# A two-block transformer on one core: later output pieces in the mixers, turns behind the next sums, and a different share of the convolution's taps

## The reference

```
def token_mixer(h, w_in, g_moba_out, g_dsa_out, w_out, cos, sin):
    proj = h @ w_in                                   # 1024 -> 3656
    mq, mk, mv, dq, dk, dv, qi, ki, wi = jnp.split(proj, offs, axis=-1)
    ...                                               # partial rope
    o_moba = moba_attention(mq, mk, mv)               # 8 heads of 64, causal (one block of 256)
    o_dsa = dsa_attention(dq, dk, dv, qi, ki, wi)     # 8 heads; each query keeps its 64 best keys
    o = jnp.concatenate([rms_norm(o_moba, g_moba_out), rms_norm(o_dsa, g_dsa_out)], axis=-1)
    return o @ w_out

def first_block(...):
    for l in range(2):
        h = rms_norm(x, g_pre_mix[l]) * (1.0 + sc_m) + sh_m
        y = token_mixer(h, ...)
        x = x + gt_m * rms_norm(y, g_post_mix[l])
        h = rms_norm(x, g_pre_ffn[l]) * (1.0 + sc_f) + sh_f
        y = conv_glu_ffn(h, ...)
        x = x + gt_f * rms_norm(y, g_post_ffn[l])

def _conv_module(h, w1, b1, wdw, bdw, lng, lnb, w2, b2):
    a, gt = jnp.split(h @ w1 + b1, 2, axis=-1)
    u = a * jax.nn.sigmoid(gt)
    u = depthwise_conv(u, wdw) + bdw                  # 31 taps per channel
    u = jax.nn.silu(_layernorm(u, lng, lnb))          # over the 1024 channels
    return u @ w2 + b2
```

## Time and profile before

| | |
|---|---|
| median of 3 runs | 2647.69 us (2647.56 to 2654.18) |
| time of the profiled execution | 2649.03 us |
| its span from first to last instruction | 2646.9 us |
| mean granted clock of TensorE | 0.981 |
| PE busy | 2513.1 us, 95% |
| DVE / ACT / POOL busy | 66% / 41% / 17% |
| mixer 0, mixer 1 | about 50 to 240, 430 to 624 us |
| convolution module | about 1206 to 1400 us |

### The profile page before, as it was taken

One profiled execution on the slowest core, in us unless ns is written; L12 is line 12 of the kernel. 1 busy time (PEld: TensorE's weight loads), 2 busy tenths in 40 slices (PEclk: granted clock), 3 DMA queues, 4 the chain that ended last, 5 costly groups with the idle time before them and its releaser, 6 DMA issues. The chain is left out here.

```text
span 2646.9 us, 35239 instructions
## 1 busy us (share of the span) xinstructions
PE 2513.1 (95%) x13530; PEld 2102.8 (79%) x13530; DVE 1739.2 (66%) x2566; ACT 1077.4 (41%) x1824; POOL 447.4 (17%) x466
## 2 busy tenths in 40 slices
PE   4899999989999999999989999999999999999998
PEld 3678997678988878878648888888888888777997
DVE  6977886966995785775865464665565765345454
ACT  3445554446554222226755322224322224334543
POOL 1101111001121121113842112101112110000111
PEclk9989999999999999999999999999999999999999
DMA  7544785534774563551102243452343353222462
GB/s 304 203 161 149 265 324 207 203 128 171 246 267 153 166 203 125 191 183 65 64 24 72 88 172 144 146 183 89 135 167 119 143 182 117 89 77 71 156 196 95
DMA packets 118294, 413.02 MB, mean 156 GB/s; under 512 B 13552, under 2 KB 17776, under 8 KB 118128
## 3 DMA queue, kind: packets, MB, share of 16 engines
q1 hardware_dynamic: 117568, 409.06, 44.4%
q10 hardware_dynamic: 560, 1.72, 0.2%
HBM read 409.68 MB, written 1.05 MB: 155 GB/s over the span
## 5 line engine op out<-in xcount | busy, mean ns | idle before, releaser
L1102 PE MATMUL ps<-hH,sh 128*128 128x256 f32 (+1 forms) x2560 | 842.6, 329 | 7.2 <-DVE sl L1672 2.8
L1103 PE MATMUL ps<-hL,sh 128*128 128x256 f32 (+1 forms) x2560 | 835.7, 326 | 0.0
L1104 PE MATMUL ps<-hH,sl 128*128 128x256 f32 (+1 forms) x2560 | 835.6, 326 | 0.0
L1672 DVE TENSOR_TENSOR sl<-raw,sh 128x1024 fp32r<-128x1024 f32 x534 | 650.6, 1243 | 119.3 <-ACT sh L1381 118.7
L1381 ACT ACTIVATE sh<-raw 128x1024 fp32r<-128x1024 f32 x534 | 540.2, 1039 | 391.5 <-PE ps L1104 317.9
L1686 DVE CUSTOM_DVE_ANT_0 mjunk<-raw,cB,V 128x1024 bf16<-128x1024 f32 x384 | 546.5, 1423 | 32.3 <-DMA C<-in_cst 8.4
L1102 PEld LDWEIGHTS ps<-hH,sh 128*128 128x128 f32 x2560 | 483.0, 189 | 59.5 <-issue 9.3
L1103 PEld LDWEIGHTS ps<-hL,sh 128*128 128x128 f32 x2560 | 481.0, 188 | 48.6 <-issue 1.7
L1104 PEld LDWEIGHTS ps<-hH,sl 128*128 128x128 f32 x2560 | 481.0, 188 | 48.1
L2167 POOL TENSOR_TENSOR uLl<-F,uHh 128x256 fp32r<-128x256 f32 (+1 forms) x132 | 165.8, 1256 | 981.9 <-ACT uHh L1561 851.7
L1102 PE MATMUL ps<-sh,uHh 128*128 128x512 f32 x792 | 314.2, 397 | 14.8 <-DVE sl L1672 14.6
(11 more groups left out here) (170 smaller groups left out, 2284.9 us busy)
## 6 DMA issues: line engine op xcount, KB each, us to landing
raw<-in_w SPq DMA_DIRECT2D x756, 512.0 KB, 4.4
raw<-in_w SPq DMA_DIRECT2D x16, 256.0 KB, 3.7
cB<-in_rpb SPq DMA_DIRECT2D x64, 64.0 KB, 2.7
X<-in_x ACTq DMA_DIRECT2D x1, 1024.0 KB, 11.8
X<-in_ctx SPq DMA_DIRECT2D x1, 1024.0 KB, 8.0
out<-X SPq DMA_DIRECT2D x2, 512.0 KB, 2.6
raw<-in_w SPq DMA_DIRECT2D x2, 288.0 KB, 6.0
cB<-in_c ACTq DMA_DIRECT2D x1, 512.0 KB, 5.6
```

What stands on the lines that cost most here:

```text
L1102: self.e.matmul(out, lh, rh, start=start, stop=False)
L1103: self.e.matmul(out, lh, rl, start=False, stop=False)
L1104: return self.e.matmul(out, ll, rh, start=False, stop=stop)
L1672: self.e.tensor_tensor(lo[:, 0:w], raw[:, 0:w], hi[:, 0:w].bitcast(F32), ALU.subtract).then_inc(self.sems["w_lo"], 1)
```

## The change

It reorders steps of the plan, and moves some of the convolution's work between engines. PE's rows of the program go from 11,805 to 11,804; DVE's stay at 2,049.

1. `index_scores`: each tile's eight rounds are four steps of `aside` with two rounds each, before two steps of four.
2. Output pieces are written to the columns of tiles 2 and 3 of h, which nothing else uses there, and are issued four rounds after their row (before: two, and none before the projection's end), one in a round. The 5-fold warm-up before the second half of the output product is gone, and row 1's DSA piece is issued behind the first evacuation.
3. `gate_half` puts the held turns out before `rms_close`; `norm_tile` has `early`, which puts the splits before the scale. The last tile of each is thus evacuated and squared before the earlier tile's turn. `down` does so only for l = 0 by `lead`, and the neighbourhood attention's output product by `early`.
4. The convolution: ACT and POOL do seven taps of a group before its next step (five of the last; before four), the last two groups have other shares, 8 warm-ups stand between the last two means (before 12 behind the last), and the groups whose hL is made by DVE are 0, 3, 5, 7 (before 1, 3, 5, 7; the rest is POOL's).

```diff
--- before.py
+++ after.py
@@ -21,7 +21,9 @@
 HALF = KF // 2
 NEG = -1e30
 GONE = -3e38
-SHARE = [(5, 11)] * 2 + [(6, 10)] * 4 + [(9, 10), (13, 8)]
+SHARE = [(5, 11)] * 2 + [(6, 10)] * 4 + [(7, 9), (13, 5)]
+HL_V = (0, 3, 5, 7)
+FIRST = [7] * 7 + [5]
 
 UNIT = 1024
 RAW = 8
@@ -213,13 +215,15 @@
     def xs(self, t, h):
         return ("x", t, h, self.x_at[(t, h)])
 
-    def norm_tile(self, hid, t, AB, s, st=None, wide=False, lag=0):
+    def norm_tile(self, hid, t, AB, s, st=None, wide=False, lag=0, early=False):
 
         if st is None:
             st = self.rms_open(self.xs(t, 0), D)
         self.rms_more(st, self.xs(t, 1))
         self.first_parts(lag)
         self.rms_close(st, 2)
+        if early:
+            self.second_parts()
         ys = [self.place("S", j) if wide else self.next("PT", 2) for j in range(2)]
         self.add("scale", t=t, st=st, ys=ys, xs=[self.xs(t, 0), self.xs(t, 1)])
         self.second_parts()
@@ -263,7 +267,7 @@
         self.left(b)
         self.add("hsplit", p=p)
 
-    def down(self, w, act, nk, k0, tiles, done, bias=None, c0=0):
+    def down(self, w, act, nk, k0, tiles, done, bias=None, c0=0, lead=False):
 
         if bias is not None:
             self.flush()
@@ -288,7 +292,7 @@
                         self.second_parts()
                     self.add("down", unit=n, ks=ks, tiles=[(i, (t, banks[i]))], last=i == len(tiles) - 1,
                              full=banks[i] if u == len(taken) - 1 else None, **common)
-                if i and len(tiles) == 2:
+                if i and lead:
                     self.first_parts()
                     self.second_parts()
                 done(t, half, banks[i])
@@ -331,6 +335,7 @@
         if half == 0:
             st2[("y", t)] = y
             return
+        self.first_parts()
         self.rms_close(st2[t], 2)
         for j in range(2):
             x0 = self.xs(t, j)
@@ -338,7 +343,7 @@
             self.add("gate2", y=(st2[("y", t)], y)[j], t=t, j=j, st=st2[t], x0=x0, x1=self.xs(t, j))
             if j == 0:
                 st = self.rms_open(self.xs(t, 0), D)
-        self.norm_tile(hid, t, AB, 0, st)
+        self.norm_tile(hid, t, AB, 0, st, early=True)
 
     def gated(self, t, half, b, gid, fast):
         f = self.next("F", 3)
@@ -402,7 +407,7 @@
                 self.left(b)
 
         h2 = self.new()
-        late, ripe = [], [False]
+        late = []
 
         def out(it, ob):
             kd, i = it["kind"], it["i"]
@@ -412,14 +417,13 @@
             self.rms_close(st, 1)
             self.add("oscale", mid=mid, kd=kd, i=i, st=st)
             A = ("V", "g_dsa_out" if kd else "g_moba_out", (l,), 0)
-            late.append([2, lambda: self.o_piece(("O1", i, 512 * kd), ("os", mid, kd, i), 4 * kd, i, A, "v", h2)])
+            late.append([4, lambda: self.o_piece(("O1", i, 512 * kd), ("os", mid, kd, i), 4 * kd, 2 + i, A, "v", h2)])
 
         def pieces(all=False):
-            for x in list(late):
+            for x in late:
                 x[0] -= 1
-                if ripe[0] and (x[0] < 0 or all):
-                    late.remove(x)
-                    x[1]()
+            if late and (all or late[0][0] < 0):
+                late.pop(0)[1]()
 
         def stream(kind):
             items = []
@@ -488,7 +492,6 @@
                     turn(("stg", stg, cb), list(range(g0, g0 + 4)), sc, g0 // 4)
             pending.append(go)
         assert not pending and not moba
-        ripe[0] = True
         gid = self.gates_later("w_ada", l, 2, ("g_post_mix", (l,)), 1)
 
         w, act, tiles = ("w_out", l), ("h", h2), [0, 1]
@@ -496,7 +499,7 @@
         units = [(kp, half) for kp in range(4) for half in range(2)]
 
         def part(kp, half, n, which, last, full=None):
-            self.add("down", unit=n, ks=[2 * kp, 2 * kp + 1], tiles=[(i, (i, banks[half][i])) for i in which], last=last,
+            self.add("down", unit=n, ks=[2 * kp, 2 * kp + 1], tiles=[(2 + i, (2 + i, banks[half][i])) for i in which], last=last,
                      full=full, act=act, nk=KD, bias=False)
 
         def take(kp, half):
@@ -516,8 +519,8 @@
             self.pace()
         self.flush()
         AB = [ab_next()]
-        self.warm(5)
-        pieces(True)
+        while len(late) > 1:
+            pieces(True)
         hid = self.new()
         st2 = {}
         self.rate = RATES["out"]
@@ -526,10 +529,9 @@
             for half in range(2):
                 for kp in (2, 3):
                     part(kp, half, taken[(kp, half)], [i], i == 1, banks[half][i] if kp == 3 else None)
-                if half:
-                    self.first_parts()
-                    self.second_parts()
                 self.gate_half(i, half, banks[half][i], gid, AB, hid, st2)
+                if i == 0 and half == 0:
+                    pieces(True)
                 self.pace()
         self.u_at += 1
         self.add("u_free", u=self.u_at)
@@ -545,8 +547,7 @@
         steps = []
         for i in range(2):
             steps += [lambda i=i: (some(i, 0), some(i, 1)), lambda i=i: (some(i, 2), some(i, 3))]
-            steps += [lambda i=i: self.add("rank", mid=mid, i=i, lo=0, hi=4),
-                      lambda i=i: self.add("rank", mid=mid, i=i, lo=4, hi=8)]
+            steps += [lambda i=i, lo=lo: self.add("rank", mid=mid, i=i, lo=lo, hi=lo + 2) for lo in range(0, 8, 2)]
         self.turn_at["S"] = -1
         self.aside[0:0] = steps
 
@@ -589,7 +590,7 @@
             AB[0] = ab_next()
         self.aside += [lambda: None] * (5 if l else 9) + [later]
         self.down(("w_down", l), ("u1", fid), KF, 0, [0, 1],
-                  lambda t, half, b: self.gate_half(t, half, b, gid, AB, hid, st2))
+                  lambda t, half, b: self.gate_half(t, half, b, gid, AB, hid, st2), lead=l == 0)
         self.flush()
         self.u_at += 1
         self.add("u_free", u=self.u_at)
@@ -693,9 +694,9 @@
             self.add("cglu_v", c=c, ba=ba, s=s, up=ups[c], cid=cid)
             self.left(ba, bu)
             if c:
-                tap_p(c - 1, 4, SHARE[c - 1][1])
+                tap_p(c - 1, FIRST[c - 1], SHARE[c - 1][1])
                 tap_v(c - 1, 5, 31)
-            tap_p(c, 0, 4)
+            tap_p(c, 0, FIRST[c])
             if 0 < c < 7:
                 tap_w(c + 1)
 
@@ -721,14 +722,13 @@
             group(c, ba, bu)
             if c == 5:
                 AB = [ab_next()]
-        tap_p(7, 4, SHARE[7][1])
         bias = ("conv_b_pw2_2", (0,))
         mean(5)
         taps(7)
         tap_v(7, 5, 31)
         mean(6)
+        self.warm(8)
         mean(7)
-        self.warm(12)
         b = self.bank()
         for c in range(KD):
             self.add("ln_sq", c=c, m=total[0], b=b, f=self.next("F", 3), cid=cid)
@@ -825,7 +825,7 @@
         def done(t, half, b):
             self.gated(t, half, b, gid, half == 1)
             if half:
-                self.norm_tile(h2, t, AB, t // 2, early[t], t % 2 == 1, 1)
+                self.norm_tile(h2, t, AB, t // 2, early[t], t % 2 == 1, 0, True)
             else:
                 early[t] = self.rms_open(self.xs(t, 0), D)
 
@@ -2054,7 +2054,7 @@
         self.wait_ge(self.got("rstd", s["cid"]))
         self.e.tensor_tensor(self.flat(c), self.flat(c), self.buf(s["b"])[:, :], ALU.mult).then_inc(self.sems["v_ps"], 1)
         self.done("v_ps", ("cn", s["cid"], c), *([("left", s["b"])] if c == KD - 1 else []))
-        if c % 2:
+        if c in HL_V:
             self.hc_lower(s, "v_sb")
 
     def hc_lower(self, s, sem):
@@ -2195,7 +2195,7 @@
             self.done("p_sb", ("left", f), *([("ap", cid, c)] if j == SHARE[c][1] - 1 else []))
 
     def ln_out(self, s):
-        if s["c"] % 2 == 0:
+        if s["c"] not in HL_V:
             self.hc_lower(s, "p_sb")
```

## The result

The changed kernel takes 2642.49 us (median of 20 runs, 2633.04 to 2648.00), the kernel before in the same rounds 2649.28 us (20 runs, 2644.94 to 2654.18). The ratio is 0.9973, with a 95% interval of 0.9964 to 0.9981: some 7 us faster, where 9.4 was forecast. The profiled execution took 2643.63 us, its span went from 2646.9 to 2641.8.

What follows compares the result with a forecast made beforehand. PE was taken as the bound, busy 2513.1 of 2646.9 us, with DVE the bound in the front. Terms -8.5 - 5.5 + 8.5 - 0.6 - 3.3 = -9.4 took the profiled 2649.0 to 2639.6, median about 2638.3; range 2628 to 2649.

Steps and rivals of the forecast that it cites:

- the forecast's 45: The 45% chance given to the forecast's own case, with a range of 2631 to 2644 us.
- Ranks, -8.5: Mixer fronts: ranks in four steps bring evacuations of q and k earlier, saving 4.0 us in mixer 0, 4.5 in mixer 1.
- The walk: Mixer 0's front: DVE's new order with old durations; PE transposes the fifth MoBA item 4.4 us earlier, the next gives 0.4 back.
- The forecast sign for the ranks: Mixer fronts: PE's waits on L1482 and L1847, 12.4 us before, would fall under 4.
- ranks only move: Rival, 20%: with DVE 96% busy in the front, a removed wait returns at a later item; 2646.8 us.
- DSA starts, -5.5: Starts of the DSA rounds: shorter waits for the copy of PT save 4.5 us, less half clock 0.5 a mixer.
- Ends, +8.5: End of attention: later pieces cost 2.3 and 1.8 us in the mixers, half clock behind an uncovered wait 4.4.
- Convolution, -3.3: Convolution: new shares, warm-ups moved between the last means, and group 0's hL on DVE together save 3.3 us.
- (a): Convolution's taps: with new shares the last CB is ready 0.2 us earlier; PE's wait of 7.76 stands.
- (b): Convolution's warm-ups: sums of squares start 5.6 us earlier but half clock costs 3.1, so -2.5, from -0.8 to -4.2.
- (c): Convolution: hL of group 0 takes 0.69 us on DVE for 1.26 on POOL, saving 0.6 us.
- Neighbourhood attention, -0.6: Neighbourhood attention: evacuation, squares and splits go ahead of PE's 1.87 us wait for a scale, saving 0.6 us.

Runs made afterwards that it cites:

- E1: The changed kernel with the ranks back in two steps of four rounds; 2644.42 us, 0.9988 of the kernel before.
- E11: E6 with MoBA row 0's piece two rounds behind its row and ranks in two steps of four rounds; 2636.56 us, 0.9970 of the kernel before.
- E3: The changed kernel with the turns ahead of the last tile's evacuation and squares again, everywhere; 2645.53 us, 0.9995 of the kernel before.
- E4: The changed kernel with all of the convolution's part undone; 2644.97 us, 0.9991 of the kernel before.
- E6: The changed kernel with only DSA's output pieces issued as before, behind the 5-fold warm-up; 2629.41 us, 0.9941 of the kernel before.
- E7: The changed kernel with a 10-fold warm-up inside the 5.4 us wait ahead of the last sums; 2637.92 us, 0.9975 of the kernel before.
- E9: E6 again, unaltered, on another chip; 2632.33 us, 0.9946 of the kernel before.
- E12: E6 without the 5-fold warm-up ahead of row 1's piece; 2638.15 us, 0.9974 of the kernel before.
- E5: The changed kernel again, unaltered, on another chip; 2643.89 us, 0.9990 of the kernel before.
- E8: The changed kernel with the convolution's 12-fold warm-up back behind the last mean; 2644.49 us, 0.9995 of the kernel before.
- E2: The changed kernel with all output pieces issued as before, and the 5-fold warm-up; 2637.75 us, 0.9963 of the kernel before.

## Why the prediction came out as it did

The time was near by luck: errors nearly as large as the whole forecast cancelled. In the first trace the ranks gave 8.3 us less than their term and the convolution 1.1 less. The DSA starts gave 4.8 more, the ends cost 4.4 less, and the neighbourhood attention gave 2 more. Stretches that the change doesn't touch took some 6 back. The gain was 6.8 us, or 2.4 on the other chip. The 57% for a gain of over 0.3% was too much even by the prediction's own account: it counted 40 of the forecast's 45 as below 2639.8, though the forecast's range goes on to 2644.

- **Ranks, -8.5: wrong.** They gave 0.9 in mixer 0 and cost 0.7 in mixer 1; E1 and E11 find nothing to tell from zero. The step that failed is "PE ... transposes that item at about 134.1 rather than 138.47 ... The next item gives 0.4 back". That item was transposed at 137.53, and the next one is 0.9 earlier too. The walk followed masks and transposes, and left out that the products with v need copies of PT from DVE. The first of these stood behind two rounds, the two operations that end the rank and a modulation step. PE, 7.5 us ahead until then, waits 3.85 us for it at 126.73 (4.56 in mixer 1), and runs at half clock for 3.6 us behind it. The forecast sign for the ranks, waits on L1482 and L1847 under 4 us, came true (1.6) without the gain. The rival "ranks only move" named it: DVE works 46.9 of 48.6 us there before and after.
- **DSA starts, -5.5: right in kind.** They gave 5.3 and 5.0. The waits themselves went from 6.1 to 4.5 us in mixer 0 and from 5.9 to 3.8 in mixer 1, 3.7 instead of 4.5. The other 6.6, for which I took 1.0, is mostly the granted clock, which rose from 0.66 to 0.86 in mixer 0; a part is that row 1's division no longer stands behind row 0's piece on DVE, which the ends pay for. That share is not the edit's alone: with the same order of instructions there, six of the experiments' kernels (E3, E4, E6, E7, E9, E12) show 0.80, E1, E5 and E8 0.86. E3, E4 and E7, whose order is that of the changed kernel up to the last division, gained 5.4 us there, just the forecast, instead of 10.3.
- **Ends, +8.5: right in place, too large.** The wait of 5.6 was 5.40, that of 1.1 was 0.85, the start 2.1 later instead of 2.2. The half clock behind it was dearer (0.86 over 25 us, 3.5 us of work, for 2.1; 0.93 in E4), and of that a filled wait gives back 1.3 to 1.7 (E7). Off was "1.5 less" for the chain behind the last sum: the last turn's wait fell by 3.2, and the half clock behind it (0.90 from 228 to 245 us) went with it. Net +2.2 and +1.9, where 4.4 and 4.1 were forecast.
- **Removing the warm-up.** E7 and E12 price it apart from lateness: 1.3 to 1.7 us a mixer in a wait of 5.4, 1.2 to 2.4 in one of 3.3 us, with the clock of 1.00 from 205 to 230 us where PE is kept busy and 0.86 where it is not. The rule of the Trainium skill ("TensorE: Matmul & The Clock Gate", Part 1: The HAM clock gate), that an idle array falls to its lower clock and returns to the full one only after work, agrees with both. A given wait doesn't always bring half clock, though: behind that of 1.9 us at 430 us the clock was 1.00 in the kernel before and 0.72 from 432 to 436 us in the changed one.
- **Convolution, -3.3: too much, -2.2, and only -0.7 against E4.** (a) The last CB comes 2.0 us later against the module's first product, where I had 0.2 earlier. PE's wait for UP at 1244.02 has grown by 0.9. DVE's 12 taps take 9.46 us (7.09 for 9 before) and begin only when PE's are done (rows of the changed kernel below). (b) From the last mean to the first product 24.1 us became 19.8; 3.6 of that is the warm-up (2.5 forecast, 4.2 the bound), and 2.1 against E4. (c) hL of group 0: 4.33 to 3.72, 0.6 as forecast.

```profile
1358.70 9.46 DVE L2027 SCALAR_TENSOR_TENSOR ps<-UP,V,ps 128x512 f32<-128x512 f32 x12 [3.75 <-PE ps L1318]
...
1368.94 2.08 PE L1330 MATMUL ps<-CB,ones 128*128 128x512 f32 x2 [5.97 <-DVE CB L2034]
```

- **Neighbourhood attention, -0.6.** Its wait went from 1.87 to 0.82. The trace shows 2.6 us, but E4, with the same order, only 1.2 of it. The other 1.4 to 1.5 lie at 2400 to 2416 us, where the change moves nothing and the clock was 0.89 for 0.80.
- **Not in the sum.** 3.2 us in the feed-forward of layer 0 (4.05 us ahead at its start, 0.87 at 418 us) and 1 in the last feed-forward, for the pace of matmuls (below). 1.4 at 431 to 437 us, for half clock. And 2.1 us in layer 1's second product, where a wait of 0.69 us for sl is new beside the old one of 1.8, with half clock behind (0.79 of 804 to 812 us, 1.00 before).

## What to carry to other kernels

When an in-order engine is 96% busy, a walk must follow every operation that another engine takes from it, to the last one of the item: here the copy of PT, the last of them, took back nearly all that PE had won by the earlier ones. A piece of work is best moved to where the busy engine has slack and nobody is near the end. Half of this change (MoBA's pieces in the projection) did that: E6 and E9 are 0.2% faster than E2, which lacks it (on other chips, with intervals that overlap), and the attention of E9 is 4 us shorter. The other half (DSA's pieces behind the last row) undid it: without it the kernel is 0.5 to 0.6% faster than before, instead of 0.1 to 0.3%. Part of that is clock that the trace of one execution doesn't show, so look at the mean clock of all of them. Ahead of a short wait of PE near the end of a stage, keep it busy, and look at PSUM banks that are handed out in turn whenever a step moves.
